# RWKV output stage: values centred at the transposes, squares and weight splits in the state loop, head tiles interleaved with the projection

## What is computed

```python
_, y = lax.scan(_rwkv7_step, state0, (r, decay, k, v, -kk, kk * a))   # y is linear in v
mu = jnp.mean(y, -1, keepdims=True)
var = jnp.mean(jnp.square(y - mu), -1, keepdims=True)
y = ((y - mu) * lax.rsqrt(var + GN_EPS)).reshape(B, S, D) * gn_w + gn_b
bonus = (jnp.sum(rh * kh * r_k, -1, keepdims=True) * vh).reshape(B, S, D)
return ((y + bonus) * g) @ w_out
```

## Time and profile before

| | us |
|---|---|
| median of 3 runs | 2702.58 |
| lowest, highest | 2698.37, 2706.6 |
| the profiled execution | 2702.59 |
| its span | 2700.8 |
| TensorE busy in the span | 2527.4 |
| DVE, ACT, POOL busy | 1302.6, 989.2, 917.4 |

### The profile page before, as it was taken

How to read it: one execution, slowest core, us unless ns; L and a number is a source line. 1 busy time by engine, 2 the same in 40 slices (tenths; PEclk the granted TensorE clock), 3 DMA queues, 4 the chain that set the end, 5 groups by cost and what they waited for, 6 DMA issues and landing times.

```text
span 2700.8 us, 34329 instructions
## 1 busy us (share of the span) xinstructions
PE 2527.4 (94%) x14232; PEld 2007.3 (74%) x14232; DVE 1302.6 (48%) x1905; ACT 989.2 (37%) x1470; POOL 917.4 (34%) x301
## 2 busy tenths in 40 slices
PE   7996666899999999999999999999999999999999
PEld 5745565378887887878888777898877777777786
DVE  5564885573434254343111434466606436676604
ACT  4652453433322233433322223332324334344523
POOL 2312331554444433453444444332243333111132
PEclk8998898999999999999999999999999999999999
DMA  6121343314555322112222542211122222111121
GB/s 268 63 78 38 85 92 93 119 63 181 189 189 203 140 94 94 48 63 78 94 93 96 198 141 97 92 65 63 70 96 92 82 91 97 63 49 61 55 94 62
DMA packets 92103, 272.13 MB, mean 101 GB/s; under 512 B 54720, under 2 KB 54848, under 8 KB 64320
## 3 DMA queue, kind: packets, MB, share of 16 engines
q1 hardware_dynamic: 89232, 255.03, 27.2%
q10 hardware_dynamic: 2736, 15.21, 1.4%
HBM read 264.44 MB, written 5.78 MB: 100 GB/s over the span
## 4 chain that ended last, share of the span: by engine, by line
PE 79%; DVE 10%; ACT 4%; issue 2%; DMA 2%; POOL 2%; SPq 0%; ACTq 0%; POOLq 0%; DVEq 0%
PE bank L348 19%; PE bank L350 19%; PE bank L349 19%; PE bank L284 2%; PE bank L282 2%; PE bank L283 2%; POOL ring_low L379 1%; ACT w_high L369 1%; PE bank L3111 1%; PE bank L3420 1%; DVE q_rope L3633 1%; PE bank L809 1%; PE bank L725 1%; PE bank L2235 1%; PE bank L3414 1%
## 5 line engine op out<-in xcount | busy, mean ns | idle before, releaser
L379 POOL TENSOR_TENSOR ring_low<-ring,w_high 128x2048 fp32r<-128x2048 f32 (+2 forms) x179 | 784.9, 4386 | 1467.6 <-ACT w_high L369 1467.6
L348 PE MATMUL bank<-h_high,w_high 128*128 128x512 f32 (+1 forms) x1304 | 520.5, 399 | 7.0 <-POOL ring_low L379 3.9
L350 PE MATMUL bank<-h_high,ring_low 128*128 128x512 f32 (+1 forms) x1304 | 517.7, 397 | 0.0
L349 PE MATMUL bank<-h_low,w_high 128*128 128x512 f32 (+1 forms) x1304 | 514.5, 395 | 0.0
L369 ACT ACTIVATE w_high<-ring 128x2048 fp32r<-128x2048 f32 (+2 forms) x184 | 331.5, 1801 | 356.3 <-PE bank L350 341.4
L348 PEld LDWEIGHTS bank<-h_high,w_high 128*128 128x128 f32 (+1 forms) x1304 | 245.2, 188 | 68.5 <-issue 6.7
L349 PEld LDWEIGHTS bank<-h_low,w_high 128*128 128x128 f32 (+1 forms) x1304 | 245.0, 188 | 60.0 <-issue 0.7
L350 PEld LDWEIGHTS bank<-h_high,ring_low 128*128 128x128 f32 (+1 forms) x1304 | 245.0, 188 | 59.5
L348 PE MATMUL bank<-z_high,w_high 128*128 128x512 f32 x384 | 154.7, 403 | 8.5 <-POOL ring_low L379 3.0
L350 PE MATMUL bank<-z_high,ring_low 128*128 128x512 f32 x384 | 153.5, 400 | 0.0
L349 PE MATMUL bank<-z_low,w_high 128*128 128x512 f32 x384 | 153.3, 399 | 0.0
(11 more groups left out here) (483 smaller groups left out, 4639.4 us busy)
## 6 DMA issues: line engine op xcount, KB each, us to landing
ring<-in_stream SPq DMA_DIRECT2D x194, 1024.0 KB, 4.8
ada_slot<-in_ada_next SPq DMA_DIRECT2D x40, 512.0 KB, 3.4
ada_slot<-in_first SPq DMA_DIRECT2D x8, 1024.0 KB, 5.5
gain_weights<-in_gains ACTq DMA_DIRECT2D x4, 2048.0 KB, 11.8
scale_weights<-in_first SPq DMA_DIRECT2D x4, 1024.0 KB, 19.2
inverse<-scratch_inverse SPq DMA_DIRECT2D x16, 256.0 KB, 4.2
w_first<-in_first SPq DMA_DIRECT2D x2, 1024.0 KB, 7.7
x_res<-in_x SPq DMA_DIRECT2D x2, 1024.0 KB, 12.1
```

The source lines that it names most:

```text
L348: pe.matmul(out, w_high[:, k, cols], x_high, start=start, stop=False)
L349: pe.matmul(out, w_high[:, k, cols], x_low, start=False, stop=False)
L350: return pe.matmul(out, w_low[:, k, cols], x_high, start=False, stop=stop)
L379: pool.tensor_tensor(self.c.ring_low[:, b % SLOTS, 0:cols], self.c.ring[:, b % SLOTS, 0:cols], self.high_buf[:, b % 2, 0:cols].bitcast(F32 ...
```

## The change

The constant `block_ones` becomes `centring`: the identity less 1/64 within a head. The values are multiplied by it where they were transposed, so that y leaves the recurrence with mean zero in each head; mean and centring go. In the state loop ACT squares each finished chunk into `f.sq` (over x, which is reloaded later), TensorE sums the squares of tokens 0 to 255 for tiles 0 to 5 after chunks 5 and 6, and the first two weight blocks of the output are split: high on ACT (`o_high`), remainder on DVE in eight pieces (`o_low`). The readouts of chunks 6 and 7 are added by DVE (`collect_late`), directly from PSUM. In the output stage the other sums follow, root and reciprocal run in two halves of the tokens, 12 warming products stand on TensorE, four tiles are spread first, and tile k + 4 is spread after the projection of tile k. POOL's gate products, remainders and weight remainders go to DVE. The diff, cut to its core:

```diff
 
-def sum_heads(chip, pe, out, n, products):
+def sum_heads(chip, pe, out, n, products, cols=slice(0, T)):
 
     a = n // 4
-    return pe.matmul(out[head_group(n), :], chip.k("head_groups")[:, 32 * a:32 * a + 32], products,
+    return pe.matmul(out[head_group(n), cols], chip.k("head_groups")[:, 32 * a:32 * a + 32], products,
                      start=(a == 0), stop=(a == 1))
...
+    f.sq = chip.over("sq", [P, KD, T], F32, chip.x_offset)
...
             mm.then_inc(av_mm.sem, 1)
             for n in range(3):
-                pe.transpose(chip.bank[5][:, n * P:(n + 1) * P], f.v[:, p, CHUNK + n * P:CHUNK + (n + 1) * P],
-                             chip.ident[:, :])
-            pe.matmul(chip.bank[5][0:64, 3 * P:], f.v[:, p, chunk(7)], chip.ident[:, :], start=True, stop=True)
-            pe.matmul(chip.bank[5][64:P, 3 * P:], f.v[:, p, chunk(0)], chip.ident[:, :], start=True, stop=True)\
+                pe.matmul(chip.bank[5][:, n * P:(n + 1) * P], f.v[:, p, CHUNK + n * P:CHUNK + (n + 1) * P],
+                          chip.k("centring"), start=True, stop=True)
+            pe.matmul(chip.bank[5][0:64, 3 * P:], f.v[:, p, chunk(7)], chip.k("centring"), start=True, stop=True)
+            pe.matmul(chip.bank[5][64:P, 3 * P:], f.v[:, p, chunk(0)], chip.k("centring"), start=True, stop=True)\
               .then_inc(av_mm.sem, 1)
 
...
                     mm.then_inc(gs_mm.sem, 1)
-                if c > 1:
+                if c == NC_ - 1:
+                    late.wait(pe, g)
+                elif c > 1:
                     os_out.wait(pe, u - 4)
                 for n in range(half_pairs):
...
                 gate_tile(3 + c, 4 + 2 * (c % 2))
+            if c in (5, 6):
+                gated.wait(pe, 6)
+                f.sq_done.wait(pe, 3)
+                for n in range(3 * (c - 5), 3 * (c - 4)):
+                    sum_heads(chip, pe, chip.bank[6], n, f.sq[:, n, 0:T // 2], slice(0, T // 2))
         pe.sem_inc(chip.gemm_done, 2)
 
...
             if p == KD:
                 gate_tile(2, 0)
+
+        def o_high(s):
+            chip.wait_block(act, b_o + s)
+            act.activation(chip.w_high[:, (b_o + s) % 2, :], chip.ring[:, (b_o + s) % SLOTS, :], ACT.Copy)\
+               .then_inc(f.o_rounded.sem, 1)
+
+        o_high(0)
         gate_tile(3, 4)
         for c in range(1, NC_):
             for g in range(2):
                 u = 2 * c + g
-                os_mm.wait(act, u - 2)
-                act.activation(f.r[:, half_pairs * g:half_pairs * (g + 1), chunk(c)],
-                               bank(2 + g, CHUNK)[:, 0:half_pairs, :], ACT.Copy).then_inc(os_out.sem, 1)
+                if c < NC_ - 2:
+                    os_mm.wait(act, u - 2)
+                    act.activation(f.r[:, half_pairs * g:half_pairs * (g + 1), chunk(c)],
+                                   bank(2 + g, CHUNK)[:, 0:half_pairs, :], ACT.Copy).then_inc(os_out.sem, 1)
+            if c < NC_ - 1:
+                summed.wait(act, 2 * c - 1)
+            else:
+                late.wait(act, 1)
+            act.activation(f.sq[:, :, chunk(c - 1)], f.r[:, :, chunk(c - 1)], ACT.Square).then_inc(f.sq_done.sem, 1)
             if c <= 4:
                 gate_tile(3 + c, 4 + 2 * (c % 2))
+            if c == 1:
+                o_high(1)
 
...
             return buf[:, half_pairs * g:half_pairs * (g + 1), :]
 
+        def o_low(n):
+            s, part_ = (b_o + n // 4) % SLOTS, slice(n % 4 * 512, (n % 4 + 1) * 512)
+            dve.wait_ge(f.o_rounded.sem, f.o_rounded.of(n // 4))
+            dve.tensor_tensor(chip.ring_low[:, s, part_], chip.ring[:, s, part_],
+                              chip.w_high[:, (b_o + n // 4) % 2, part_].bitcast(F32), ALU.subtract)\
+               .then_inc(f.o_rest.sem, 1)
+
+        def collect_late(c):
+            for g in range(2):
+                os_mm.wait(dve, 2 * c + g - 2)
+                dve.tensor_tensor(f.r[:, half_pairs * g:half_pairs * (g + 1), chunk(c)],
+                                  bank(2 + g, CHUNK)[:, 0:half_pairs, :],
+                                  f.nkk[:, half_pairs * g:half_pairs * (g + 1), chunk(c)], ALU.add)\
...
             if c <= 4:
+                o_low(2 * c - 2)
                 bonus_tile(3 + c, 4 + 2 * (c % 2))
+                o_low(2 * c - 1)
                 gated_tile(3 + c, 4 + 2 * (c % 2))
+        collect_late(NC_ - 2)
         ada_sum.wait(dve, KD - 1)
         ada_finish(chip, dve, 3 * KD, 5 * KD, ada_biased, ada_one_plus)
+        collect_late(NC_ - 1)
 
     def gpsimd(pool):
...
         y2_mm.wait(pool, KD - 1)
-        for c in range(1, NC_):
+        for c in range(1, NC_ - 1):
             for g in range(2):
                 u = 2 * c + g
                 here = slice(half_pairs * g, half_pairs * (g + 1))
-                if c < NC_ - 1:
-                    state.wait(pool, u - 2)
-                    pool.tensor_tensor(Tm[:, here, :], (X1, Y1)[(c - 1) % 2][:, here, :], f.k[:, here, chunk(c)],
-                                       ALU.add).then_inc(base.sem, 1)
+                state.wait(pool, u - 2)
+                pool.tensor_tensor(Tm[:, here, :], (X1, Y1)[(c - 1) % 2][:, here, :], f.k[:, here, chunk(c)],
+                                   ALU.add).then_inc(base.sem, 1)
                 if c > 1:
                     collect(pool, u - 2)
-        for g in range(2):
...
-    var_mm, root, inverse = Step(chip, "rw_var", KD), Step(chip, "rw_root", 1), Step(chip, "rw_inverse", 1)
-    with_gate_dve, with_gate_pool = Step(chip, "rw_with_gate_dve", 4), Step(chip, "rw_with_gate_pool", 4)
+    sq_done, var_mm = Step(chip, "rw_sq", 1), Step(chip, "rw_var", 2)
+    root, inverse = Step(chip, "rw_root", 2), Step(chip, "rw_inverse", 2)
+    with_gate = Step(chip, "rw_with_gate", KD)
...
 
     def tensor(pe):
-        for n in range(KD + 2):
-            if n < KD:
-                if n >= 2:
-                    pe.wait_ge(centred.sem, centred.of(n - 2))
-                pe.matmul(chip.bank[4 + n % 2][:, :], chip.k("block_ones"), f.r[:, n, :], start=True, stop=True)\
-                  .then_inc(mean_mm.sem, 1)
-            if n >= 2:
-                pe.wait_ge(sq_done.sem, sq_done.of(n - 2))
-                sum_heads(chip, pe, chip.bank[6], n - 2, sq[:, (n - 2) % 4, :]).then_inc(var_mm.sem, 1)
-        pe.wait_ge(centred.sem, centred.of(KD - 1))
-        pe.wait_ge(inverse.sem, inverse.of(0))
+        for n in range(6, KD):
+            mm = sum_heads(chip, pe, chip.bank[6], n, f.sq[:, n, 0:T // 2], slice(0, T // 2))
+        mm.then_inc(var_mm.sem, 1)
         for n in range(KD):
+            sum_heads(chip, pe, chip.bank[5], n, f.sq[:, n, T // 2:T - CHUNK], slice(T // 2, T - CHUNK))
+        pe.wait_ge(sq_done.sem, sq_done.of(0))
+        for n in range(KD):
+            mm = sum_heads(chip, pe, chip.bank[5], n, f.sq[:, n, T - CHUNK:T], slice(T - CHUNK, T))
+        mm.then_inc(var_mm.sem, 1)
+        chip.keep_warm(pe, 12)
+
+        def spread_tile(n):
             if n >= 4:
                 pe.wait_ge(unit.sem, unit.of(n - 4))
             spread_heads(chip, pe, chip.bank[spread_bank[n % 4]][:, :], n, rows).then_inc(spread.sem, 1)
+
+        pe.wait_ge(inverse.sem, inverse.of(1))
+        for n in range(4):
+            spread_tile(n)
         for s in range(2):
-            split.wait(pe, b_o + s)
+            pe.wait_ge(f.o_rest.sem, f.o_rest.of(4 * s + 3))
             chip.wait_pair(pe, u_o + s)
-        parts = [split.parts(b_o + s, KD, 2 * P) for s in range(2)]
+        parts = [[a[:, :].rearrange("p (k n) -> p k n", k=KD)
+                  for a in (chip.w_high[:, (b_o + s) % 2, :], chip.ring_low[:, (b_o + s) % SLOTS, :])] for s in range(2)]
         for k in range(KD):
             pe.wait_ge(z_rest.sem, z_rest.of(k))
             for m in range(4):
@@ -1900,30 +1948,26 @@
                            (z_high[:, k, :], z_low[:, k, :]), k == 0, k == KD - 1)
                 if k == KD - 1:
                     mm.then_inc(chip.gemm_done, 1)
+            if k + 4 < KD:
+                spread_tile(k + 4)
         chip.pe_features(pe, b_o + 2, u_o + 2, 2, KD, lambda k: (z_high[:, k, :], z_low[:, k, :]), split=split_last)
         tail.tensor(pe)
 
     def scalar(act):
+        last = slice(T - CHUNK, T)
+        act.activation(f.sq[:, :, last], f.r[:, :, last], ACT.Square).then_inc(sq_done.sem, 1)
         act.dma_start(g1[:, :, :], chip.io["gains"][0, 0, 1]).then_inc(g1_in.sem, 16)
+        for n, cols in enumerate(halves):
+            act.wait_ge(var_mm.sem, var_mm.of(n))
+            act.activation(rows[:, cols], chip.bank[6 - n][:, cols], ACT.Sqrt, bias=chip.gn_eps[:, :], scale=1.0 / HEAD)\
+               .then_inc(root.sem, 1)
         act.dma_start(chip.x[:, :, :], chip.io["x"].rearrange("(k p) t -> p k t", p=P)).then_inc(x_back.sem, 16)
-        split.high(act, b_o)
-        for n in range(KD):
-            act.wait_ge(centred.sem, centred.of(n))
-            if n >= 4:
```

(59 more changed lines are left out.)

27 lines of the change are left out of this document (14 added, 13 removed).

## The result

The changed kernel takes 2686.23 us (median of six runs, 2681.17 to 2689.06), the kernel before 2701.68 us beside it (six runs, 2698.37 to 2706.6). The ratio is 0.9937, 95% interval 0.9925 to 0.9949: 15.5 us off the medians, faster by more than 0.3%. The profiled execution took 2687.94 us with a span of 2686.2 us and a mean granted clock of 0.971; before it was 2702.59, 2700.8 and 0.967.

A forecast was written before the change was run, and what follows sets the result against it. The prediction took TensorE's chain as the bound, with 31.8 us of latency before the output projection. Its terms, -22.3 + 4.3 + 1.0 + 2.5 + 2.4 = -12.1 us, took 2702.6 to 2690.5 us, range 2684 to 2696.5.

The forecast's parts named there:

- Stage start, -0.6 us: End of the state loop: with POOL's collect gone, the output stage starts at 512.7 instead of 513.28.
- The loop's new work, 0.2 us in all: State loop: DVE's weight remainder pieces fit idle time, costing 0.2 us in all; ACT's added work costs 0.
- DVE and POOL hold each other up in the loop: Rival, state loop: the two engines block each other, 1.6 us in all, giving 2692.1 us; chance 0.13.
- The prologue, 31.8 to 10.1 us: Output stage before its projection: the projection starts at 522.8 instead of 545.1, -22.3 us.
- The table load, 1.28 us: ACT's table load before the root: costs its row's 1.28 us, without about 1.38 us of added drain.
- Four spreads between the tiles, +4.3: Inside the projection: TensorE does four spreads between tiles, 1.07 us each at the higher clock, +4.3 us.
- One spread caught at the lower clock, +1.0: Start of the projection: one spread falls in the stretch at the lower clock, another +1.0 us.
- the first matmuls at it, 0 more: Start of the projection: the same clock fall as before, 12.4 matmuls losing 2.4 us, so 0 more.
- The boundary wait, +2.5: Between the projection's halves: TensorE waits for banks behind DVE's 13.75 us queue, against 11.2 us of matmuls, +2.5 us.
- A second climb of the clock behind it, +2.4: Between the projection's halves: the clock falls again in TensorE's wait, one more climb of 12.4 matmuls, +2.4 us.
- the clock holds at the boundary: Rival, between the projection's halves: no clock fall in the short wait, 2688.1 us; chance 0.18.
- After the projection everything is as before.: Everything behind the projection: unchanged, only earlier, so no cost.

The follow-up runs named there:

- experiment 1: Kernel before, with only the three value transposes a pair made products with the identity: 2701.61 us against 2703.63, ratio 0.9988.
- the second profile of the change: Changed kernel run again unaltered, in another job beside the kernel before: median 2689.69 us, ratio 0.9943.
- experiment 2: Changed kernel with squares and early sums moved from the state loop to the head of the output stage: 2693.49 us, ratio 0.9951.
- experiment 3: Changed kernel with the first two weight blocks split at the output stage's head again, remainders on POOL: 2695.55 us, ratio 0.9957.
- experiment 6: Changed kernel with ten products of 128 columns put between the first spreads and the projection: 2689.66 us, ratio 0.9940.
- experiment 8: Changed kernel without its twelve warming products before the first spreads: 2687.66 us, ratio 0.9927.
- experiment 9: Changed kernel with the remainders of the projection's last two weight blocks back on POOL: 2687.39 us, ratio 0.9931.
- experiment 4: Changed kernel with all eight spreads ahead of the projection, none between its tiles: 2685.85 us, ratio 0.9928.
- experiment 7: Changed kernel with gain rows moved behind tiles 4 to 7 and ten products ahead of the projection: 2682.52 us, ratio 0.9921.
- experiment 5: Changed kernel with DVE's four gain rows moved behind tiles 4 to 7: 2681.7 us, ratio 0.9916; run again, 2686.86 us, ratio 0.9935.

## Why the prediction was right, point by point

The time, 2690.5 us forecast and 2686.23 measured, is inside the range of 2684 to 2696.5, and "faster by over 0.3%" had most of the chance. The prologue, the spreads and the boundary wait came as written, the terms of the clock did not; these are the terms.

- **Stage start, -0.6 us.** In the trace -2.7 (513.28 to 510.56), but 2.3 of them were there before the loop began, where the change adds only the hidden products of experiment 1. From 400 to 430 us the clock was at 0.94 before and 1.00 after, in stretches with nearly the same work:

```profile
400.00:430.00 30.00, 19.95 (x467) 18.22 (x467) 22.51 (x44) 14.11 (x33) 6.84 (x4) 0.94 0.38 74
```

```profile
400.00:430.00 30.00, 20.36 (x525) 18.70 (x527) 24.21 (x47) 13.99 (x33) 6.82 (x4) 1.00 0.35 75
```

  The loop's start lies anywhere from 479.6 to 487.2 in the profiles of versions whose code up to there is the same, so these 2.3 us are chance of two executions. The clock's fall is not shown to be the reason: the second profile of the change has 1.00 in the same stretch too, and starts its loop at 483.77. The change's own part is -0.4 against -0.6.
- **The loop's new work, 0.2 us in all.** Right. The rounds are still 5.12 us. DVE's pieces fit, and even one that lies beside POOL costs nothing that the loop's 29.46 us (29.88 before) shows:

```profile
500.46 0.91 POOL L1831 TENSOR_TENSOR rw_all<-rw_all 128x256 f32<-128x256 f32 x1
...
500.70 1.22 DVE L1758 TENSOR_TENSOR ring_low<-ring,w_high 128x512 fp32r<-128x512 f32 x1
```

  The rival "DVE and POOL hold each other up in the loop" is thus half true: the hold is there, 0.5 us for such a piece (0.68 us for one that lies free), and the slack takes it, as it was said to take most of it.
- **The prologue, 31.8 to 10.1 us.** 9.93: the term that carries the change, right to 0.2 us, and each of its steps can be read in the chain above. Experiments 2 and 3 show two of its parts by undoing them, 3.6 and 5.5 us in the traces, 2 to 4 and 4 to 5 us in the times. The rest, some 13 us, is by the rows of the two chains the mean and centring rounds, the locked gate product and the spreads; no experiment undid them, so for this largest part the cause is read from the traces and not tested.
- **The table load, 1.28 us.** The load ends at 512.46 and its user starts at 512.48; the square ahead of it ends at 511.17 and the load starts at 511.18:

```profile
511.18 1.28 ACT L1962 ACT_TABLE_LOAD   x1
...
512.48 0.84 ACT L1962 ACTIVATE gn_rows<-bank,gn_eps 128x256 f32<-128x256 f32 x2
```

  Keeping the row's price was right. The Trainium skill (ScalarE: Activation LUTs, What ACT_TABLE_LOAD costs) adds 1.38 us of drain, which no row here shows on either side of the load; the measurement decides.
- **Four spreads between the tiles, +4.3.** Under-sized. The instructions take 1.07 us as forecast, but the matmuls' starts tell the cost: a tile with a spread ahead of it takes 4.00 us (525.99 to 529.99), one without 12 x 0.232 = 2.78. So 1.2 each, 4.8: the pauses of the array on either side belong to it.
- **One spread caught at the lower clock, +1.0; the first matmuls at it, 0 more.** The fall came where it was expected and was shorter. After, the clock was at half for 3.3 us of the projection, 8 matmuls, 1.5 us lost, where before 12.4 matmuls had lost 2.4; no spread was caught. Together -0.9 instead of +1.0.
- **The boundary wait, +2.5.** 2.33 us, for the reason given. Its feed, 4.40 + 4.59 + 1.42 us on the chain, is the queue written out in the forecast, and the gain rows were not stretched: 1.22 us each, with POOL idle, where the earlier trace rows had one of 5.65 beside it.
- **A second climb of the clock behind it, +2.4.** It came in this profile at 1.5 us (8 matmuls), and not at all in the second profile of the same program nor in experiment 6. Seven profiles have a boundary wait of 2.3 us or more, and the clock was at half behind it in five: this one, experiments 2, 3 and 8 (8 or 9 matmuls each) and experiment 9 (14 matmuls behind 3.22 us). So the forecast was right to hold it for the likelier case and mostly too high in its size. The rival "the clock holds at the boundary", 2688.1, describes the other two.
- **"After the projection everything is as before."** Wrong by +2.5 us in this profile: the clock fell in the tail, while TensorE did products of one column and of 128. After, by timeline:

```profile
578.21 1.36 PE L556 MATMUL bank<-ones,tail_squares 128*128 128x1 f32 x8
579.43 1.20 PE L201 MATMUL bank<-ones,ident 128*128 128x128 f32 x4
580.42 1.91 PE L562 MATMUL bank<-ident,tail_cols 128*128 128x128 f32 x8
582.13 3.62 PE L201 MATMUL bank<-ones,ident 128*128 128x128 f32 x16
```

  The last of these took 1.95 us before. Of the eleven profiles of versions with this part, seven fell in it and four did not (experiments 4, 7, 9 and the first of 5); of the two with the stage as before (the kernel before, experiment 1) neither did. Why was only seen and not tested.

**The sum.** The terms that belong to the program, prologue with its start, spreads and wait, were -22.3 + 4.3 + 2.5 = -15.5 in the forecast, and are -0.4 - 21.9 + 4.8 + 2.3 = -15.2 in the traces. For the clock the forecast added 1.0 + 2.4 = 3.4, and the traces have -0.9 + 1.5 + 2.5 = 3.1, with one place of the three not foreseen and both foreseen ones too large. That makes -12.1 on both sides, and that the clock's part agrees so well is luck: its terms are 1.0, 2.4 and nothing in the forecast, -0.9, 1.5 and 2.5 in the traces. What is left between the forecast of 2690.5 and the profiled 2687.94 are the 2.3 us ahead of the loop and 0.35 us elsewhere, which are chance; the median of the six runs lies another 1.7 us lower. In the other job the medians are 14.8 us apart, so the forecast is some 3 us high in both, about the size of its clock terms: it may be that the profiled executions had more falls in this part than an average one, which stays an inference, since only profiled runs show where the clock falls.

The other rivals: DVE was not the bound of the projection (all its instructions there 0.69, 2.24 and 1.22 us); the change does what it says; and the clock did not stay at 1.2 GHz, though four spreads stood between the tiles: from 524 to 550 it was at 1.00.

## What to carry to other kernels

Latency in front of a dense stage goes one for one to the end, and a sum of instruction durations along its chain gave it to 0.2 us; small work put under a neighbouring loop's idle time really vanishes. But ask what the pipelining itself puts into the dense part: spreads between the tiles, a wait where the freed engine's work has gone to another, and a clock that may fall in each. Here these gave back all that the interleaving had won, and an order without it is as fast. Whether it pays once the wait is designed away is open: experiment 5 had 2681.7 us beside the 2685.85 of experiment 4 in one job, but its ratios, 0.9916 and 0.9935, lie on either side of experiment 4's 0.9928. On DVE, what stands ahead of the urgent piece in the queue counts as much as what the piece waits for.

## What the runs showed of the hardware

- The clock falls at different places in executions of one program. With the granted clock and the time of each run side by side: the changed kernel 2681.17 us at 0.974 and 2689.06 at 0.971; experiment 7's version 2673.16 at 0.977 and 2686.65 at 0.969. Over the last pair 0.008 of the clock goes with 13.5 us, 1.7 us for 0.001; 0.001 of 2686 us is 2.7 us of full clock lost, so part of a fall lies under waits that are there anyway. The spread of 8 us between runs of one kernel goes with the clock, and a difference of 2 us between kernels drowns in it.
- The Trainium skill (TensorE: Matmul & The Clock Gate, Part 1: The HAM clock gate) says that how many matmuls run at the lower clock differs from run to run of one kernel (its example is 6, 11 or 14 of them). The traces agree: behind the same boundary wait of 2.33 us, 8 matmuls in one profile of the changed kernel and none in the other.
- The dense transfers of the prologue (share 0.92, 345 GB/s from 510.5 to 520.4) show no delay of an engine's instructions: the squares and gate products in it keep their 0.63 and 0.69 us.
- POOL needs 4.5 us for a remainder of 2048 elements and DVE 2.24 (540.82, two in 4.48), so taking them from POOL cost DVE half of what POOL was rid of.
